# When the loads, a row store and the read-back around the expert routing are asked for, in a hybrid decoder layer on one core

## The chip, the cores and the metric

One NeuronCore of a Trainium2 chip runs the whole layer in float32. The metric is device time in microseconds (us) of one execution, lower is better; the kernel before is given as the median of three timed executions, and one more execution was profiled.

## The reference

A decoder layer over 1024 tokens of width 1024: conditioning by `c`, input projection, sparse attention beside differential attention, output projection, and then a mixture of 32 experts. Only the last part matters here:

```python
x = x + gate_a[:, None] * jnp.dot(o, w_out[l])             # the residual that is kept
h = rms_norm(x, g_moe[l]) * (1.0 + scale_m) + shift_m
# hier_moe: top-1 group of 4, then top-2 of its 8 experts; gates from two softmaxes
for e in range(N_EXPERTS):
    hid = jax.nn.silu(jnp.dot(h, w_gate[e])) * jnp.dot(h, w_up[e])
    y = y + gates[:, e:e + 1] * jnp.dot(hid, w_down[e])
x = x + gate_m[:, None] * y
return rms_norm(x, g_final)
```

## The kernel before, in words

**Stages.** Conditioning and projections, the two attentions, then three stages that matter here.

*Output projection and routing.* For each of T = 8 row tiles of 128 tokens, TensorE (PE) projects (`project_out`), VectorE (DVE) adds the residual into `XT` (the tile `X`, 8 x 1024 columns), ScalarE (ACT) writes the tile scaled by its root mean square into `h2` (L954, signal `h2_done`), PE turns the tile and ACT keeps it in `h2T`, and PE computes the router's logits from `h2T` (L1985, signal `lg_ps`). `h2` has two places, `SC[0:2048]`, and `h2T` two, `SC[2048:4096]`. Each row tile of `h2` is stored to the DRAM tensor `h2_rows` by SyncE's queue (SP, `store_h2`, L533, signal `h2_out`). From the logits, DVE and PE build a list of token rows: 20 steps of 128 rows, each step four slots of 32 rows for one expert a slot. The list is `lst` (L1452, signal `route_done` 1). While DVE works on the list PE runs matmuls without a use (`keep_warm`, L1944): 5, then 6, then 14 of them, each two instructions. After the 14, PE waits for `route_done` and for the first gathered rows.

*Experts.* For step n GpSimd (POOL) gathers 128 rows of `h2_rows` into one of two places `xg` (L707, an indirect DMA), PE turns them (L2011), ACT and DVE scale them (L969, L1538), PE multiplies by gate and up (L2024), ACT and DVE form the hidden rows (L977, L1519, L1521), PE turns them (L2033) and multiplies by down (L2047), DVE multiplies by `out_row` (L1529) and POOL scatters the result to `expert_rows` (L714). The first `ev_hid` of DVE waits for `out_row`. POOL starts the first two gathers once it has `route_done` and both counts of `h2_out` (L738 to L742); the third waits until PE has turned the first.

*Weights.* Every expert's weights come from HBM once: gate 1 MB and up 1 MB into one of 7 gate/up places, down 1 MB into one of 7 down places, all by SP's queue in a written-out order. Expert w (in the order of `SEQ`) uses place w % 7. Place 6 for gate/up is `SC[0:4096]`: gate lies in the columns of `h2`, up in those of `h2T`. Place 4 for gate/up and for down and place 5 for down lie in `X`: columns 0 to 6143 are free after the last use by expert 25, the rest after that by expert 26. Experts 23 to 25 are last used in step 15, expert 26 in step 17, experts 29 to 31 in step 19. Expert 6 is first used in step 3. A place is asked for again when PE has finished with it: gate/up after `gu_ps` (L580), down after `dn_ps` (L584). So the loads of experts 7 and 8 are the first of a stream that begins when PE has finished gate/up of step 0.

*End.* The residual was overwritten by weights, so SP reads it back as `h2_rows` into `XT` (L587 to L589, signal `x2_back`, waited for as 8 tiles by PE at the end and by DVE). When all scatters have landed (`rows_out`) SP reads the 8 MB of `expert_rows` into `yg` (L614), PE and DVE add them to the residual, ACT, POOL and DVE normalise, and SP stores the output (L617).

**The order on SP around the change** (L559 to L577): wait for the end of the projection; gate/up of expert 5; down 2; wait for `h2_done` 8 and store the last row tile; down 3; wait for `h2T_ps`; down 5; wait for both `h2_out`; wait for `lg_ps` 8; gate and up of expert 6; wait for `route_done` 1 and for the first two gathers (`xg_in`); `out_row`; down 6; then the loop over the steps.

Of the kernel before, what the change touches and what calls it, by code (L numbers as in the profile page):

```python
# [14 lines left out]
P = 128  # L15
# [9 lines left out]
def groups_of(i):  # L25

    kind, _, t = tile_at(i)
    step = 4 if kind == "diff" else 2
    return [(b, min(b + step, t + 1)) for b in range(0, t + 1, step)]
# [36 lines left out]
def hybrid_layer(nc, x, c, w_ada, b_ada, g_attn, w_in, g_kv, w_uk, w_uv, lam_q1, lam_k1, lam_q2, lam_k2,  # L66
                 g_sub, w_out, g_moe, w_group, b_group, w_router, b_router, w_gate, w_up, w_down, g_final, out):
    _, S, D = x.shape
    T = S // P
    KC = D // P  # L70
    _, NH, LAT, DH = w_uk.shape
    DV = g_sub.shape[1]
    QD = lam_q1.shape[1]
    NG = w_group.shape[2]
    NE = w_router.shape[2]
# [21 lines left out]
    DNS = 7  # L97
# [26 lines left out]
    parts, last_use = [], {}  # L124
# [24 lines left out]
    h2_dram = nc.dram_tensor("h2_rows", [S, D], F32, kind="Internal").ap()  # L149
# [4 lines left out]
    with ctx:  # L154
# [3 lines left out]
        def sem(name):  # L158
            return ctx.enter_context(nc.semaphore(name))
# [117 lines left out]
        h2 = SC[:, 0:2 * D].rearrange("p (a n) -> p a n", a=2)  # L277
# [28 lines left out]
        def dist(t):  # L306
# [42 lines left out]
        op_ps, x2_sq, h2_done = (  # L349
            sem(n) for n in ("op_ps", "x2_sq", "h2_done"))  # L350
        h2_out = [sem(f"h2_out{i}") for i in range(2)]
# [4 lines left out]
        gu_in = [sem(f"gu_in{i}") for i in range(GUS)]  # L356
# [11 lines left out]
        gu_at = [QKV[:, 0:4096], QKV[:, 6144:10240], QKV[:, 20480:24576], W7[:, :], X[:, 0:4096],  # L368
                 QKV[:, 12288:16384], SC[:, 0:4096]]
# [42 lines left out]
        wg_d = w_gate[0].rearrange("e (p c) n -> e p (c n)", c=KC)  # L412
        wu_d = w_up[0].rearrange("e (p c) n -> e p (c n)", c=KC)
# [1 line left out]
        x_d = x[0].rearrange("(t p) d -> t p d", p=P)  # L415
        win_d = w_in[0].rearrange("(j p) n -> p j n", p=P)

        def gate_up_load(sp, e, b):

            for dst, src in ((gu_at[b][:, 0:2048], wg_d), (gu_at[b][:, 2048:4096], wu_d)):  # L420
                sp.dma_start(dst, src[bass.ds(e, 1)].rearrange("o p n -> (o p) n")).then_inc(gu_in[b], 16)

        def down_load(sp, e, b):

            sp.dma_start(dn_at[b], wd_d[bass.ds(e, 1)].rearrange("o p n -> (o p) n")).then_inc(dn_in[b], 16)
# [23 lines left out]
        def _(sp):  # L449
# [80 lines left out]
            def store_h2(t):  # L530

                sp.wait_ge(h2_done, t + 1)
                sp.dma_start(h2_dram[P * t:P * (t + 1), :], h2[:, t % 2, :]).then_inc(h2_out[t % 2], 16)  # L533

            def expert_of(w):

                sp.wait_ge(eid_done, 1)
                return sp.value_load(eid[0:1, SEQ[w]:SEQ[w] + 1], min_val=0, max_val=NE - 1)

            def freed(n, places):  # L540

                return [w for w in range(places, NE) if last_use[w - places] == n]

            for t in range(SPILLED):
                if t == 1:
                    sp.wait_ge(op_ps, 2)
                    sp.dma_start(gate_late, mod_dram[:, 0:D].partition_broadcast(P).rearrange(
                        "p o (k n) -> p (o k) n", k=KC)).then_inc(out_row_in, 16)
                elif t == EARLY + 1:
                    for w in range(IN_X):  # L550
                        gate_up_load(sp, expert_of(w), w)
                        down_load(sp, expert_of(w), w)
                    sp.wait_ge(op_sb, 2 * EARLY)
                    for w in range(IN_X, IN_X + 2):
                        gate_up_load(sp, expert_of(w), w)
                store_h2(t)
            sp.wait_ge(h2T_ps, 2 * SPILLED)
            gate_up_load(sp, expert_of(4), 4)
            down_load(sp, expert_of(4), 4)  # L559
            store_h2(SPILLED)  # L560
            sp.wait_ge(op_ps, 2 * T)
            gate_up_load(sp, expert_of(5), 5)
            down_load(sp, expert_of(2), 2)
            store_h2(T - 1)
            down_load(sp, expert_of(3), 3)
            sp.wait_ge(h2T_ps, 2 * T)
            down_load(sp, expert_of(5), 5)
            for i in range(2):
                sp.wait_ge(h2_out[i], 16 * (T // 2))
            sp.wait_ge(lg_ps, T)  # L570
            gate_up_load(sp, expert_of(6), 6)
            sp.wait_ge(route_done, 1)
            for i in range(2):
                sp.wait_ge(xg_in[i], 16)
            sp.dma_start(out_row, mod_dram[:, 3 * D:4 * D].partition_broadcast(P).rearrange("p o n -> p (o n)")
                         ).then_inc(out_row_in, 16)
            down_load(sp, expert_of(6), 6)  # L577
            for n in range(NSTEP + 1):
                if n < NSTEP:
                    sp.wait_ge(gu_ps, n + 1)  # L580
                    for w in freed(n, GUS):
                        gate_up_load(sp, expert_of(w), w % GUS)
                if n >= 1:
                    sp.wait_ge(dn_ps, 2 * n)  # L584
                    for w in freed(n - 1, DNS):
                        down_load(sp, expert_of(w), w % DNS)
                    if n - 1 == last_use[max(range(5, NE, DNS))]:  # L587
                        for t in range(T):
                            sp.dma_start(XT[:, t, :], h2_dram[P * t:P * (t + 1), :]).then_inc(x2_back, 16)  # L589
            sp.wait_ge(route_done, 2)  # L590
            n_ov = sp.value_load(ovi[0:1, NOV:NOV + 1], min_val=0, max_val=NOV)
# [30 lines left out]
        def _(pool):  # L622
# [64 lines left out]
            for i, t in enumerate(sel_tiles):  # L687
                w = P * (t + 1)
                sc = SC[:, sc_off[t]:sc_off[t] + w]
                above, _, run = (a[:, 0:w] for a in sel_tmp[i % 2])  # L690
                pool.wait_ge(sel_kept, i + 1)
                link(pool.tensor_tensor(run, run, above, ALU.add))
                link(pool.tensor_scalar(run, run, -1.0, -NEG, ALU.add, ALU.mult))
                pool.tensor_tensor(sc, run, dist(t), ALU.add).then_inc(sel_done, 1)
# [73 lines left out]
        def _(act):  # L768
# [66 lines left out]
            for n in range(IH * NS):  # L835
                t = sel_tiles[n // IH]
# [11 lines left out]
            for step in range(32):  # L848
                act.wait_ge(trial_set, step + 1)
                for k in range(ONACT):  # L850
                    i, n = ONDVE + k, ONACT * step + k
                    t = sel_tiles[i]
                    w = P * (t + 1)
# [67 lines left out]
            for i in range(NA):  # L921
                n = len(groups_of(i))
# [17 lines left out]
            for t in range(T):  # L940
                act.wait_ge(x2_half, 2 * t + 2)
                if t:
                    act.wait_ge(x2_sq, t)
                if t >= 2:
                    act.wait_ge(h2_out[t % 2], 16 * (t // 2))
                act.activation(h2[:, t % 2, :], XT[:, t, :], ACT.Square, accum_out=ss[:, 2 * T + t:2 * T + t + 1]
                               ).then_inc(x2_sq, 1)
                for h in range(2):
                    act.wait_ge(h2T_ps, 2 * t + h + 1)
                    if t >= 2:  # L950
                        act.wait_ge(lg_ps, t - 1)
                    act.activation(h2T[:, t % 2, BANK * h:BANK * (h + 1)], PS[:, 4 + h, :], ACT.Copy).then_inc(h2T_sb, 1)
                act.wait_ge(rstd_done, rstd_x2 + t + 1)
                act.activation(h2[:, t % 2, :], XT[:, t, :], ACT.Copy, scale=ss[:, 2 * T + t:2 * T + t + 1]  # L954
                               ).then_inc(h2_done, 1)
            act.wait_ge(e2_in, 1)
            act.activation(gx[:, :, :], gx[:, :, :], ACT.Exp).then_inc(route_exp, 1)
            act.wait_ge(e2_in, 2)
# [37 lines left out]
            with act.If(n_ov > 0):  # L996
                with act.Fori(0, NOV // 2) as i:
                    for b in range(2):
                        with act.If(n_ov > 2 * i + b):
                            n = 2 * i + (NSTEP + b)  # L1000
# [8 lines left out]
            for t in range(T):  # L1009
                if t in mixed:  # L1010
                    i = mixed.index(t)
# [1110 lines left out]
```

## Time and profile before

| | us |
|---|---|
| median of three timed executions | 1015.87 (1013.1 to 1015.96) |
| the profiled execution, its own time | 1011.23 |
| its span, first to last instruction | 1009.4 |

| engine | busy in the span |
|---|---|
| PE matmul | 953.4 us, 94% |
| DVE | 594.8 us, 59% |
| ACT | 400.8 us, 40% |
| POOL | 119.0 us, 12% |

189.88 MB were moved by DMA at a mean of 188 GB/s over the span, and at some 420 GB/s from about 730 us to 940 us. The mean granted clock of TensorE was 0.987 of full speed. Times in rows are us from the start of the span. PEld is TensorE's weight load; "SPq" is an instruction of SP's queue, with the time that it took to issue and not the time to landing. In a row with an arrow in brackets, the number is how long the engine had been idle and the name behind the arrow is what ended it. A window's row has, after the busy time of each engine, PEclk (1.00 is the 2.4 GHz level, 0.50 the 1.2 GHz level), the mean busy share of the DMA engines, and GB/s.

### The profile page before, as it was taken

The page shows a single profiled execution, that of the slowest core. Times are in us where ns is not written, and L with a number is a line of the kernel's source. Part 1 is how long each engine was busy: PE and PEld are TensorE (multiplying, and loading weights), DVE is VectorE, ACT ScalarE, POOL GpSimd, SP SyncE. Part 2 cuts the span into 40 slices and gives each one's busy share as a digit, 9 for nine tenths or more (in the row PEclk, how much of TensorE's full clock was granted, in tenths as well). Part 3 has the DMA queues.
Part 4 walks back from the last instruction along what each step waited for, and adds up shares of the span by engine and source line. Part 5 has one row for each costly group of instructions (what it writes and reads, how often), then busy time and mean ns, then how long its engine had stood idle before and what let it go on. Part 6 is the DMA issues. An engine that isn't in the chain of part 4 may idle for free.

```text
span 1009.4 us, 15052 instructions
## 1 busy us (share of the span) xinstructions
PE 953.4 (94%) x5352; PEld 520.2 (52%) x5352; DVE 594.8 (59%) x1597; ACT 400.8 (40%) x909; POOL 119.0 (12%) x218
## 2 busy tenths in 40 slices
PE   3899999999999999999999999999899999989984
PEld 2464575444448756677766455557433434323421
DVE  3489647999999798987777234365322223312227
ACT  6130236666650488777668121212211112211113
POOL 2001000000008411110000000000111111111004
PEclk9999999999999999999999999997999999999998
DMA  9997101111111000050000410199699999999889
GB/s 325 333 358 274 43 22 32 32 42 25 39 43 27 1 1 2 1 190 2 1 2 1 167 63 22 46 412 385 252 406 421 421 417 421 420 421 419 339 334 365
DMA packets 70381, 189.88 MB, mean 188 GB/s; under 512 B 10200, under 2 KB 37136, under 8 KB 58016
## 3 DMA queue, kind: packets, MB, share of 16 engines
q1 hardware_dynamic: 62320, 171.06, 44.4%
q0 software_dynamic: 5760, 16.78, 4.2%
q10 hardware_dynamic: 2224, 1.05, 0.4%
q8 instruction: 44, 0.72, 0.3%
q14 instruction: 33, 0.27, 0.1%
HBM read 174.17 MB, written 18.89 MB: 191 GB/s over the span
## 4 chain that ended last, share of the span: by engine, by line
PE 65%; DVE 20%; DMA 6%; issue 4%; SPq 2%; ACT 1%; POOL 1%; POOLq 0%; DVEq 0%; ACTq 0%
PE PS L2024 12%; PE PS L1901 11%; DVE BIAS L1161 8%; PE PS L2047 6%; PE PS L1794 6%; PE PS L1837 5%; PE PS L1859 4%; DMA X<-in_w_down_dram 3%; PE PS L1755 3%; PE PS L1707 3%; PE PS L1854 2%; DVE X L1225 2%; PE PS L1732 2%; PE PS L2011 2%; PE PS L1672 1%
## 5 line engine op out<-in xcount | busy, mean ns | idle before, releaser
L1707 PE MATMUL PS<-HT,X 128*128 128x512 f32 x384 | 168.8, 593 | 0.0
L2024 PE MATMUL PS<-QKV,HT 128*32 128x512 f32 (+2 forms) x560 | 116.0, 607 | 6.3 <-DMA X<-in_w_up_dram 3.9
L1707 PEld LDWEIGHTS PS<-HT,X 128*128 128x128 f32 x384 | 72.5, 190 | 92.4 <-issue 92.2
L873 ACT ACTIVATE X<-X,nmx 128x128 f32<-128x128 f32 (+7 forms) x128 | 98.4, 770 | 51.6 <-DVE nmx L1225 51.0
L1901 PE MATMUL PS<-QKV,HT 128*128 128x512 f32 x256 | 113.7, 597 | 0.0
L1161 DVE TENSOR_SCALAR_CACHE_REDUCE BIAS<-SC,W 128x384 f32<-128x384 f32 (+3 forms) x128 | 96.4, 810 | 1.1
L1519 DVE TENSOR_TENSOR HT<-PS,HT 128x256 f32<-128x256 f32 x20 | 8.5, 425 | 147.8 <-ACT HT L977 147.8
L856 ACT ACTIVATE X<-SC,W 128x896 f32<-128x896 f32 x64 | 69.6, 1088 | 43.1 <-DVE W L1149 43.1
L1794 PE MATMUL PS<-QKV 64*128 64x512 f32 (+3 forms) x384 | 79.0, 517 | 1.6 <-DVE nmx L1225 1.1
L1901 PEld LDWEIGHTS PS<-QKV,HT 128*128 128x128 f32 x256 | 47.4, 190 | 53.7 <-issue 53.6
L1837 PE MATMUL PS<-ident,X 128*128 128x128 f32 x432 | 63.2, 279 | 2.2 <-DVE X L1243 2.1
L977 ACT ACTIVATE HT<-PS 128x256 f32<-128x256 f32 x20 | 7.7, 384 | 138.7 <-PE PS L2024 138.7
L2024 PEld LDWEIGHTS PS<-QKV,HT 128*32 128x32 f32 (+2 forms) x560 | 32.7, 119 | 53.8 <-issue 50.3
L1225 DVE CUSTOM_DVE_ANT_0 X<-PS,R 128x128 f32<-128x128 f32 (+7 forms) x80 | 50.8, 674 | 14.6 <-PE PS L1794 8.6
L2047 PE MATMUL PS<-QKV,HT 128*32 128x512 f32 (+2 forms) x272 | 56.2, 616 | 2.9 <-DMA X<-in_w_down_dram 2.4
L1837 PEld LDWEIGHTS PS<-ident,X 128*128 128x128 f32 x432 | 47.2, 141 | 11.4 <-issue 8.7
L1225 DVE CUSTOM_DVE_ANT_0 X<-PS,SC 128x1024 f32<-128x1024 f32 (+5 forms) x48 | 42.0, 887 | 17.9 <-PE PS L1794 17.8
L2024 PE MATMUL PS<-W,HT 128*32 128x512 f32 (+2 forms) x144 | 51.0, 619 | 0.0
L1529 DVE TENSOR_TENSOR HT<-PS,R 128x512 f32<-128x512 f32 x40 | 27.7, 692 | 32.3 <-PE PS L2047 28.4
L1794 PEld LDWEIGHTS PS<-QKV 64*128 64x128 f32 x384 | 31.6, 185 | 27.8 <-issue 20.4
L2024 PE MATMUL PS<-X,HT 128*32 128x512 f32 (+1 forms) x128 | 44.1, 609 | 0.0
L1053 DVE SCALAR_TENSOR_TENSOR QKV<-QKV,cact 128x512 f32<-128x512 f32 x56 | 42.1, 752 | 2.0
(306 smaller groups left out, 1533.7 us busy)
## 6 DMA issues: line engine op xcount, KB each, us to landing
QKV<-in_w_down_dram SPq DMA_DIRECT2D x20, 1024.0 KB
QKV<-in_w_gate_dram SPq DMA_DIRECT2D x19, 1024.0 KB
QKV<-in_w_up_dram SPq DMA_DIRECT2D x19, 1024.0 KB
QKV<-in_w_ada_dram SPq DMA_DIRECT2D x8, 2048.0 KB, 14.5
QKV<-in_w_ada_dram SPq DMA_DIRECT2D x8, 1024.0 KB, 12.8
X<-in_w_in_dram SPq DMA_DIRECT2D x16, 512.0 KB, 3.8
X<-in_w_down_dram SPq DMA_DIRECT2D x8, 1024.0 KB, 28.0
QKV<-expert_rows SPq DMA_DIRECT2D x16, 512.0 KB, 10.7
```

The costliest lines, as they stand in the source:

```text
L856: act.activation(RL[:, n % 2, 0:w], SC[:, sc_off[t]:sc_off[t] + w], ACT.Sign, bias=tk[:, 4, i:i + 1].bitcast(F32), scale=-1.0, accum_out=c ...
L873: act.activation(sc, sc, ACT.Exp, bias=nmx[:, i % 4, m:m + 1], scale=-1.0, accum_out=rs[:, i, m:m + 1]).then_inc(exp_done, 1)
L1053: link(dve.scalar_tensor_tensor(out=w[:, 0, :], in0=w[:, j, :], scalar=cact[:, j:j + 1], in1=w[:, 0, :], op0=ALU.mult, op1=ALU.add))
L1161: dve.tensor_scalar(BIAS[:, i % 3, 0:w], SC[:, sc_off[t]:sc_off[t] + w], thr.bitcast(F32)[:, i:i + 1], 0.0, ALU.is_lt, ALU.add, accum_out= ...
L1225: dve.tensor_tensor_reduce(sc_buf[i % 4][:, m, 0:w], PS[:, 2 * m:2 * m + 2, :].rearrange("p a n -> p (a n)")[:, BANK * n:BANK * n + w], aw ...
L1707: end = pe.matmul(PS[:, 2 * b + half, :], WS[:, b, j, :], HT[:, j, BANK * half:BANK * (half + 1)], start=(j == 0), stop=(j == KC - 1))
L1794: end = pe.matmul(PS[:, 2 * m + n + c0 // BANK, 0:c1 - c0], QKV[rows_m, q0:q0 + P], QKV[rows_m, k0 + c0:k0 + c1], start=True, stop=True)
L1837: end = pe.transpose(PS[:, 4 + g % 2, c0:c0 + P], sc_buf[i % 4][:, m, P * b:P * (b + 1)], ident[:, :])
L1859: end = pe.matmul(PS[DH * m:DH * (m + 1), 6 + h % 2, slot], vd[:, b, v0:v0 + DH], turned_at(i)[:, g % 4, c0:c0 + P], start=(b == 0), stop= ...
L1901: end = pe.matmul(PS[:, n % 4, :], HT[:, k, P * (n // 2):P * (n // 2 + 1)], wo[:, k, BANK * (n % 2):BANK * (n % 2 + 1)], start=(k == 0), s ...
L2024: end = pe.matmul(PS[at, 2 + b, :], hgT[b][:, P * c_ + at.start:P * c_ + at.stop], WGU[w][:, c_, :, :], start=(c_ == 0), stop=(c_ == KC - 1))
L2047: end = pe.matmul(PS[at, 5 + h, :], hidT[b][:, P * c_ + at.start:P * c_ + at.stop], WDN[w][:, c_, BANK * h:BANK * (h + 1)], start=(c_ == 0 ...
```

## The change

Four edits, all in who asks for a transfer and when. No computation changes.

1. The store of the last row tile of `h2` moves from SP's queue to ACT's, right behind the ACT instructions that make it. SP keeps the wait for `h2_done` 8, now behind down 3 instead of ahead of it.
2. SP's wait for both `h2_out` moves from ahead of the loads of expert 6 to behind its waits for the first two gathers.
3. Of expert 6's gate/up place, up (the half in the columns of `h2T`) is still asked for behind `lg_ps` 8; gate (the half in the columns of `h2`) is asked for behind the first two gathers and `out_row`.
4. The read-back of the residual is asked for in two steps: 6 tiles behind the down loads that the end of step 15 frees, 2 tiles at the end of step 17, instead of all 8 at the end of step 17.

```diff
-        def gate_up_load(sp, e, b):
+        def gate_up_load(sp, e, b, halves=(0, 1)):
-            for dst, src in ((gu_at[b][:, 0:2048], wg_d), (gu_at[b][:, 2048:4096], wu_d)):
-                sp.dma_start(dst, src[bass.ds(e, 1)].rearrange("o p n -> (o p) n")).then_inc(gu_in[b], 16)
+            for h in halves:
+                sp.dma_start(gu_at[b][:, 2048 * h:2048 * (h + 1)], (wg_d, wu_d)[h][bass.ds(e, 1)].rearrange("o p n -> (o p) n")
+                             ).then_inc(gu_in[b], 16)
...
             gate_up_load(sp, expert_of(5), 5)
-            down_load(sp, expert_of(2), 2)
-            store_h2(T - 1)
-            down_load(sp, expert_of(3), 3)
+            for w in range(2, 4):
+                down_load(sp, expert_of(w), w)
+            sp.wait_ge(h2_done, T)
             sp.wait_ge(h2T_ps, 2 * T)
             down_load(sp, expert_of(5), 5)
-            for i in range(2):
-                sp.wait_ge(h2_out[i], 16 * (T // 2))
             sp.wait_ge(lg_ps, T)
-            gate_up_load(sp, expert_of(6), 6)
+            gate_up_load(sp, expert_of(6), 6, (1,))
             sp.wait_ge(route_done, 1)
             for i in range(2):
                 sp.wait_ge(xg_in[i], 16)
+            for i in range(2):
+                sp.wait_ge(h2_out[i], 16 * (T // 2))
             sp.dma_start(out_row, mod_dram[:, 3 * D:4 * D].partition_broadcast(P).rearrange("p o n -> p (o n)")
                          ).then_inc(out_row_in, 16)
+            gate_up_load(sp, expert_of(6), 6, (0,))
             down_load(sp, expert_of(6), 6)
...
-                    if n - 1 == last_use[max(range(5, NE, DNS))]:
-                        for t in range(T):
+                    back = {last_use[25]: range(0, 6), last_use[26]: range(6, T)}
+                    if n - 1 in back:
+                        for t in back[n - 1]:
                             sp.dma_start(XT[:, t, :], h2_dram[P * t:P * (t + 1), :]).then_inc(x2_back, 16)
...
+            act.wait_ge(h2_done, T)
+            act.dma_start(h2_dram[P * (T - 1):P * T, :], h2[:, (T - 1) % 2, :]).then_inc(h2_out[(T - 1) % 2], 16)
             act.wait_ge(e2_in, 1)
```

## Rows read from the trace of the kernel before

**Rows 1.** Chain of waits, 690 to 740 us (start, us, what).
```profile
693.87 3.63 PE PS L1985 x16
...
709.38 6.08 DMA HT<-h_rows,SC
...
715.59 1.14 PE PS L2011 x8
...
718.37 8.41 PE PS L2024 x64
...
729.54 7.07 PE PS L2024 x64
```
**Rows 2.** Timeline of PE and of POOL, 694 to 742 us.
```profile
708.09 6.29 PE L1944 MATMUL PS<-HT,ident 128*128 128x256 f32 x28
...
711.00 0.99 POOL L707 DMA_INDIRECT HT<-h_rows,SC  x1 [0.31 <-issue]
```
**Rows 3.** Timeline of SP's queue, 695 to 730 us.
```profile
695.00 0.33 SPq L533 DMA_DIRECT2D h_rows<-SC  x1
...
705.09 0.34 SPq L421 DMA_DIRECT2D SC<-in_w_gate_dram  x1
705.53 0.38 SPq L421 DMA_DIRECT2D SC<-in_w_up_dram  x1
716.77 0.33 SPq L575 DMA_DIRECT2D R<-modulation_row  x1
...
727.86 0.35 SPq L421 DMA_DIRECT2D QKV<-in_w_gate_dram  x1
```
**Rows 4.** Windows, 690 to 727 us.
```profile
690.00:709.40 19.40, 17.71 (x111) 15.67 (x110) 12.68 (x57) 3.60 (x7) 0.80 (x3) 0.74 0.97 375
709.40:716.70 7.30, 6.08 (x32) 4.99 (x30) 0.86 (x5) 0.00 (x0) 2.28 (x2) 1.00 0.73 277
717.00:722.00 5.00, 3.63 (x24) 1.01 (x28) 2.87 (x14) 2.60 (x5) 0.99 (x1) 0.66 0.73 243
722.00:727.00 5.00, 5.00 (x50) 1.44 (x40) 0.00 (x0) 0.19 (x1) 0.00 (x0) 1.00 0.46 178
```
**Rows 5.** Page, what DMA moved in 40 slices of 25.2 us.
```profile
GB/s 325 333 358 274 43 22 32 32 42 25 39 43 27 1 1 2 1 190 2 1 2 1 167 63 22 46 412 385 252 406 421 421 417 421 420 421 419 339 334 365
```
**Rows 6.** Waits, 880 to 972 us (who waited for whom: sum, times, longest).
```profile
PE PS L2024 <- DMA X<-in_w_up_dram: 3.9, 1, 3.9
PE PS L2047 <- DMA X<-in_w_down_dram: 2.4, 1, 2.4
```
**Rows 7.** Waits of SP's queue, 690 to 760 us.
```profile
SPq L574 <- DMA HT<-h_rows,SC: 10.8, 1, 10.8
SPq L537 <- DMA h_rows<-SC: 6.6, 1, 6.6
```
**Rows 8.** Timeline of ACT, 694 to 742 us.
```profile
708.67 0.23 ACT L957 ACTIVATE gx<-gx 128x32 f32<-128x32 f32 x1 [13.70 <-DVE gx L1455]
```
**Rows 9.** Line 2024, its matmuls on place 6 (form, ns min/median/max, first and last start).
```profile
L2024 PE MATMUL PS<-SC,HT x112: 592/592/643, 753.8 to 937.1; 128*32 128x512 f32 x96, 128*64 128x512 f32 x16
```
**Rows 10.** Timeline of SP's queue and of PE, 917 to 974 us.
```profile
919.37 2.54 SPq L421 DMA_DIRECT2D W<-in_w_up_dram  x1
922.74 9.79 SPq L425 DMA_DIRECT2D QKV<-in_w_down_dram  x3
953.92 4.14 SPq L589 DMA_DIRECT2D X<-h_rows  x8
...
969.78 3.70 PE L2085 MATMUL PS<-X,ident 128*128 128x512 f32 x8 [0.58 <-DMA X<-h_rows]
```
**Rows 11.** Chain of waits, 893 to 975 us.
```profile
893.57 31.12 DMA X<-in_w_down_dram
...
954.23 7.00 PE PS L2024 x64
...
970.74 3.32 DMA expert_rows<-HT,SC
```

## The prediction

> **What bounds the kernel now.** I read the chain of waits first, around the change. With the list of rows ready, POOL's first gather is issued at 709.38 us and lands 6.08 us later, at 715.46; PE starts to turn the rows at 715.59, multiplies by gate and up of step 0 from 718.37 for 8.41 us, and step 1 follows at 729.54 [rows 1]. So the first gather is on the path. Then the timeline of PE: what it does meanwhile is the filler of 14, from 708.09 for 6.29 us, to 714.38 [rows 2]. PE could not turn earlier than 714.38 however soon the rows came. The idle time that a faster gather can take away is 715.59 - 714.38 = 1.21 us, and no more.
>
> Next the stretch behind it. From about 733 us DMA moves 417 to 421 GB/s slice after slice [rows 5], and PE waits for weights twice near the end of that stretch, 3.9 and 2.4 us [rows 6]. The load that ended the second wait was asked for at 893.57 and took 31.12 us [rows 11]: a queue of 31.12 x 0.42 = 13 MB stood before it. The middle of the expert part is therefore bound by the stream of weights, and the stream begins at 727.86, when PE has done gate and up of step 0 and its places are asked for again [rows 3]. What moves the end of step 0's gate/up moves the stream and everything behind it, one for one, as long as the DMA engines are free when it begins.
>
> Last the tail: SP asks for the expert rows when the last scatter has landed, 970.74 + 3.32 = 974.1 [rows 11]. Only what moves that scatter moves the tail.
>
> **Part 1, the loads ahead of the gather (edits 1 to 3).** Removed from ahead of the gathers: gate of expert 6, 1 MB, asked for at 705.09 [rows 3]. Also removed: SP's wait of 6.6 us for the row store [rows 7], so that up of expert 6 is asked for at about 697.6, when the last logits are done (693.87 + 3.63 [rows 1]), instead of 705.53, and down 3 and down 5 come a little sooner. How much is queued when the gather starts? From 709.4 to 716.7, when the second gather lands, DMA moved 7.3 x 277 = 2.02 MB [rows 4]. Two gathers are 1.05 MB, so 0.97 MB were loads still waiting. Before 709.4 DMA was 97% busy [rows 4], so asking sooner alone gains nothing; it is the 1.05 MB taken out that empties the queue, just in time. With it empty the two gathers have 0.97 / 0.42 = 2.3 us less ahead of them. The second lands at 714.4, and the first, 1.2 us ahead of it as before, at 713.2, an issue-to-landing of 3.8 us.
>
> That price has no row of its own. The bounds are 3.32 us, a scatter of the same size with little else in flight [rows 11], and 5.7 us, the second gather itself (711.00 [rows 2] to about 716.7, the end of SP's wait [rows 3, 7]), most of whose time was behind the last loads already. At 3.8 the gather lands 1.2 us inside the filler; at 5.7 it lands at 715.1. I take 3.8, nearer to the lower end, since the loads left were over half of what stood ahead. The gain is 1.2 us at 3.8, and (6.08 - 5.7) = 0.4 us at 5.7.
>
> By the Trainium skill ("DMA: Bandwidth & Descriptors", the anatomy of one DMA on the GpSimd path) such a transfer costs about 2.0 us plus its bytes at 436 GB/s, which is an estimate of 3.2 us for 512 KB. The sum would be 1.2 us by that too; the scatter's 3.32 agrees with it and the gather's 5.7 does not.
>
> **The clock.** In 717 to 722 us the granted clock was 0.66 on average: it fell to the 1.2 GHz level behind PE's 1.21 us of waiting, a turn of 1.14 us, and 1.6 us of waiting for ACT and DVE [rows 1, 4]. Gate/up of step 0 took 8.41 us, that of step 1, at the full level, 7.07: the fall costs 1.34 us [rows 1]. The change removes the first of the two waits, not the second. From below the gain is 0, from above 1.34. Between gate/up of step 0 and of step 1 (726.8 to 729.54) PE has breaks too and keeps the clock; what is left here stands between the two cases. I leave it at 0 in the sum and make the other value a rival.
>
> **What is added behind the gather.** Gate 6 (1.05 MB, 2.5 us of DMA) now stands between `out_row` and down 6, asked for at about 715. Expert 6 is first multiplied at 753.8 [rows 9], so it has 38 us. `out_row` is asked for no later than before, and DVE needs it only behind step 0's gate/up, at 727. The one thing that could be hit is the start of the stream. DMA was idle for 27% of 717 to 722 and for 54% of 722 to 727 [rows 4], 4.1 us, and 0.9 us more to 727.86; a stream that begins 1.2 us sooner leaves 3.8, against 2.5 needed. Cost 0. Without that cover it would be up to 2.5.
>
> **The store on ACT's queue (edit 1).** One issue on ACT, about 0.35 us as SP's issues are, in a gap of 13.70 us [rows 8]; behind it only the two exponentials wait, due at 708.67. Cost 0. POOL needs the store landed before it issues at 709.38. On SP's queue it took from 695.00 to about 704, where SP's wait of 6.6 us ended [rows 3, 7], behind the loads asked for before it. It has 13.5 us from 695.2, so 0; if it were held until the SP queue had drained (about 709) it would land near 710.5 and cost up to 2 us. By the Trainium skill (same page, "Issuing engines are not separate DMA queues") transfers of different engines share the same DMA engines and interleave, so the move itself saves nothing and the store is not held; no row of before has a store on ACT's queue.
>
> **SP's waits.** `h2_done` now stands behind down 3, and nothing but down 5 and up 6 is queued behind it; both had to wait for that anyway. The wait for `h2_out` behind the gathers is met on arrival, since the gathers themselves needed it.
>
> **Part 2, the read-back (edit 4).** Six of eight tiles (3.15 MB, 7.5 us) are asked for behind the down loads freed by step 15, issued from 922.74 for 9.79 us, so near 932 instead of 953.92 [rows 10]. They queue behind the last weights and fill DMA time of which the page shows some to spare (339 GB/s in the slice from 933) [rows 5]. What was late: PE's first addition of the residual waited 0.58 us [rows 10]. But its next additions wait for the last scatter, landed at 974.1 [rows 11], and 969.78 + 3.70 = 973.5 was already sooner. The last scatter took 3.32 us, our lower bound. Gain 0, from above 0.3 us.
>
> **Sum.** 1.2 + 0 + 0 = 1.2 us less. Against the profiled execution: 1011.23 - 1.2 = 1010.0 (span 1009.4 to 1008.2). That execution lies 4.6 us under the median of the timed ones, so I carry the difference and not the level: 1015.87 - 1.2 = 1014.7.
>
> **Rivals.** (a) *The clock holds too*: 1.2 + 1.34 = 2.5 us less, 1013.3. For it: only one break is left. Against: that one was the longer. 0.26. (b) *The gather is slow by itself*, 5.7 us: 0.4 us less, 1015.5; in effect the change does not do what it says. For it: the second gather. 0.18. (c), on the other side: *The read-back takes DMA time from the last weights*: up of expert 31 was asked for at 919.37; with the lag of 31.12 it lands at about 950.5, and step 19 wants it at 954.23 [rows 10, 11]. If the 3.15 MB went ahead of or among the weights, all would land 7.5 us later, of which 3.7 over the margin, and 1.3 more for a fall of the clock. It decides once over 3.7 us (1.6 MB) of read-back pass in front. Then + 5.0 - 1.2: 1019.7. Against it: the same queue of SP carries both, weights first. 0.08. (d) Something not in these rows, more often a gain (a wait on the stream that shrinks) than a loss: 0.12. My forecast case: 0.36.
>
> **Range and chances.** A measurement of this kernel tells about 0.3%, 3.05 us, from no change; the three timed executions alone span 2.9 us. (a) less 1.5 gives 1011.8, (b) plus 1.5 gives 1017.0. Over 3.05 us faster: part of (a) and (d), and little of the forecast, 0.27. Slower: (c) and a little of (b) and (d), 0.11. Within: 0.62.
>
> **What would show it.** Right: in the profile after, PE's idle time ahead of the first turn is gone or under 0.2 us; the first gather takes 3.5 to 5 us; SP asks for `R` sooner than 716.77; gate/up of step 0 takes 8.4 (forecast) or 7.1 us (rival a); the distance from its end to the end of the span is the same within 0.5 us. Wrong: a gather of over 5.5 us (b); a wait of PE on `W`, `QKV` or `BIAS` weights between 935 and 965 us (c); POOL's first gather issued later than some 0.9 us behind the list (the store); DMA still full when the stream begins.

## The result, and the profile after

| | before | after |
|---|---|---|
| median of six timed executions each, us | 1015.91 (1013.1 to 1016.11) | 1008.36 (1007.32 to 1010.08) |
| profiled execution, own time, us | 1011.23 | 1009.45 |
| its span, us | 1009.4 | 1007.7 |

The ratio is 0.9934 with a 95% interval of [0.9917, 0.9951]: 7.5 us less by the medians, where 1.2 were forecast. Two later jobs with the unchanged after gave 0.9951 [0.9935, 0.9967] and 0.9962 [0.9948, 0.9977], so some 0.5%, 4 to 7.5 us, is the size to explain. All three ratios lie beyond the 0.3% from which a gain was to be told, though the interval of the last reaches down to 0.23%. Here and below ratios are of fast executions alone; two slow ones, 1245.56 us with the read-back alone and 3218.31 us with both halves behind the gathers, are left out of them.

The two profiled spans differ by 1.7 us only. The two executions were not alike ahead of the change: the last logits start at 697.12 in the one after, at 693.87 in the one before [rows 1], and nothing that PE waits for was changed before that point. So the traces are compared from that start on. First the chain of waits after, 690 to 740 us (start, us, what), the part that answers to [rows 1]:

```profile
697.12 3.35 PE PS L1990 x16
...
711.04 5.19 DMA HT<-h_rows,SC
...
716.37 1.14 PE PS L2016 x8
...
719.16 7.12 PE PS L2029 x64
```

and PE's own timeline, with its idle time before an instruction in brackets:

```profile
709.76 6.29 PE L1949 MATMUL PS<-HT,ident 128*128 128x256 f32 x28
716.37 1.13 PE L2016 MATMUL PS<-ident,HT 128*128 128x128 f32 x8 [0.33 <-DMA HT<-h_rows,SC]
719.16 7.07 PE L2029 MATMUL PS<-QKV,HT 128*32 128x512 f32 x64 [1.66 <-ACT HT L974]
```

Three things are to be seen. The gather takes 5.19 us instead of 6.08. PE's wait for it is 0.33 instead of 1.21 us, where the prediction wanted none or under 0.2. Gate/up of step 0 takes 7.07 instead of 8.4 us. And one thing was not in the prediction at all: from the start of the last logits to the gather's issue it is 711.04 - 697.12 = 13.9 us, against 709.38 - 693.87 = 15.5 before. That stretch computes the token list. The change puts one issue into it, in a gap of ACT, and its length turns out to differ between executions of one kernel.

SP's queue after, 695 to 730 us, which answers to [rows 3]:

```profile
701.21 0.34 SPq L421 DMA_DIRECT2D SC<-in_w_up_dram  x1
718.04 0.33 SPq L576 DMA_DIRECT2D R<-modulation_row  x1
719.13 0.34 SPq L421 DMA_DIRECT2D SC<-in_w_gate_dram  x1
720.25 0.34 SPq L426 DMA_DIRECT2D BIAS<-in_w_down_dram  x1
727.02 0.34 SPq L421 DMA_DIRECT2D QKV<-in_w_gate_dram  x1
```

Up of expert 6 is asked for 4.1 us behind the start of the last logits, where it was 705.53 - 693.87 = 11.7 us; gate comes behind the gathers; the stream of weights begins at 727.02. The DMA engines just before that:

```profile
723.00:727.00 4.00, 4.00 (x39) 1.62 (x32) 0.18 (x1) 0.38 (x1) 0.00 (x0) 1.00 1.00 409
```

They were 100% busy up to the stream's start, where in the kernel before they had been 46% busy in 722 to 727 [rows 4]. "DMA still full when the stream begins" was one of the prediction's signs of being wrong.

ACT issues the store of the last row tile in 0.35 us, in a gap of 12.13 us; the store landed 8.5 us later, at about 707, well ahead of the gather's issue:

```profile
698.24 0.35 ACTq L960 DMA_DIRECT2D h_rows<-SC  x1
710.34 0.23 ACT L962 ACTIVATE gx<-gx 128x32 f32<-128x32 f32 x1 [12.13 <-DVE gx L1460]
```

Toward the end, PE's waits from 880 to 972 us, which answer to [rows 6]:

```profile
PEld PS L2090 <- DMA X<-h_rows: 4.9, 1, 4.9
PE PS L2090 <- DMA X<-h_rows: 4.0, 1, 4.0
PE PS L2029 <- DMA X<-in_w_up_dram: 3.9, 1, 3.9
PE PS L2052 <- DMA X<-in_w_down_dram: 1.3, 1, 1.3
```

The stream still makes PE wait for as long as before (3.9 us), as it should if both moved together; the wait for down is 1.3 instead of 2.4 us. The read-back, asked for 21 us sooner against the end of the last down matmul, is waited for longer than before, not shorter. Edit 4 is not the reason: in two later profiles without it, the gate half alone and edits 1 to 3 again, the wait is as long.

```profile
PE PS L2087 <- DMA X<-h_rows: 4.4, 1, 4.4
PE PS L2089 <- DMA X<-h_rows: 4.6, 1, 4.6
```

### The profile page after: what moved, and what is told of

Same layout as the page of the kernel before. It is cut to its first block, busy times and chain, and to the rows that moved or that the text cites. A ratio compares the mean times of both kernels' runs of the same rounds, so it can differ in the third digit from the quotient of the medians.

```text
span 1007.7 us, 15056 instructions
## 1 busy us (share of the span) xinstructions
PE 954.2 (95%) x5352; PEld 521.1 (52%) x5352; DVE 594.5 (59%) x1597; ACT 400.9 (40%) x909; POOL 118.2 (12%) x218
## 4 chain that ended last, share of the span: by engine, by line
PE 65%; DVE 20%; DMA 6%; issue 4%; SPq 2%; ACT 1%; POOL 1%; POOLq 0%; DVEq 0%; ACTq 0%
PE PS L2029 12%; PE PS L1906 11%; DVE BIAS L1166 8%; PE PS L2052 6%; PE PS L1799 6%; PE PS L1842 5%; PE PS L1864 4%; DMA X<-in_w_down_dram 3%; PE PS L1760 3%; PE PS L1712 3%; PE PS L1859 2%; DVE X L1230 2%; PE PS L1737 2%; PE PS L1677 2%; PE PS L2016 2%
## 5 line engine op out<-in xcount | busy, mean ns | idle before, releaser
L2029 PE MATMUL PS<-QKV,HT 128*32 128x512 f32 (+2 forms) x560 | 115.6, 599 | 6.3 <-DMA X<-in_w_up_dram 3.9
L2029 PEld LDWEIGHTS PS<-QKV,HT 128*32 128x32 f32 (+2 forms) x560 | 32.7, 117 | 53.7 <-issue 50.2
L2052 PE MATMUL PS<-QKV,HT 128*32 128x512 f32 (+2 forms) x272 | 54.5, 595 | 1.8 <-DMA X<-in_w_down_dram 1.3
## 6 DMA issues: line engine op xcount, KB each, us to landing
QKV<-in_w_up_dram SPq DMA_DIRECT2D x19, 1024.0 KB, 20.9
```

What stands on the lines that cost most here:

```text
L2029: end = pe.matmul(PS[at, 2 + b, :], hgT[b][:, P * c_ + at.start:P * c_ + at.stop], WGU[w][:, c_, :, :], start=(c_ == 0), stop=(c_ == KC - 1))
L2052: end = pe.matmul(PS[at, 5 + h, :], hidT[b][:, P * c_ + at.start:P * c_ + at.stop], WDN[w][:, c_, BANK * h:BANK * (h + 1)], start=(c_ == 0 ...
```

## The experiments

Two theories stood first: the gain is at the start of the expert part (the gather and the clock), or it is in the tail (the read-back). Every job, of two to four kernels, also ran executions of before on the same chip; ratios are against those.

**The kernel before, again.** No edit.

> The kernel before, unchanged, for a second profile. The median of before (1015.9) is 4.7 us above its profiled execution (1011.23), and the change measured 7.5 us, six times the forecast. Theory 1 (clock): the usual execution of before has more falls of TensorE's clock than the profiled one, so this profile shows a time near 1015.9 and, against the first, 2 to 5 us more at the 1.2 GHz level, with the waits on DMA the same. Theory 2 (tail): the usual execution loses its extra time behind the last down matmul, where the read-back, the last scatters and the reads of the expert rows meet: the distance from there to the end, 40.2 us in the first profile, is then 43 us or more. Time against before: the same.

Ratio 1.0004 [0.9986, 1.0022]. Its profiled execution took 1013.9 us of span, 4.5 more than the first profile of the same kernel. The granted clock in 40 slices of 25 us (page), in the first profile and in the second:

```profile
PEclk9999999999999999999999999997999999999998
PEclk9999999999999899999999999997999999999998
```

One window, in the first and in the second:

```profile
345.00:355.00 10.00, 9.44 (x53) 5.14 (x51) 9.24 (x44) 9.17 (x38) 1.89 (x6) 1.00 0.00 1
345.00:355.00 10.00, 10.00 (x35) 5.66 (x37) 7.38 (x33) 7.87 (x33) 1.29 (x3) 0.51 0.00 0
```

At 345 us, in the attention, the granted clock of the second profile was 0.51 for ten us, the 1.2 GHz level; in the first it was 1.00. By the last logits this execution was 2.9 us later (696.81 against 693.87). Theory 1 named this; the tail was 41.6 us against 40.2, not the 43 of theory 2. Over two jobs 67 executions of the kernel before took 1009.5 to 1019.0 us, and the profiled one was among the luckier. Where the clock falls is part of that scatter; whether it is all of it was not tried. It is no gain: it hits both kernels.

**The read-back alone** (edit 4 in the kernel before).

```diff
-                    if n - 1 == last_use[max(range(5, NE, DNS))]:
-                        for t in range(T):
+                    back = {last_use[25]: range(0, 6), last_use[26]: range(6, T)}
+                    if n - 1 in back:
+                        for t in back[n - 1]:
```

> Before, with edit 4 alone: read-back in two steps. Theory 1 (the gain is at the start of the expert part: gather and clock): within 1 us of before, 1015 to 1016. Theory 2 (the gain is in the tail): 4 to 6 us less, 1010 to 1012. Prediction on record: 0 to 0.3 us less.

Ratio 1.0007 [0.9995, 1.002]: nothing that can be told, as the prediction said. But its trace held the key to the rest. Here the list was early, and the old order of loads stood unchanged (chain, 690 to 735 us; PE's waits in the same stretch):

```profile
709.44 8.74 DMA HT<-h_rows,SC
718.31 1.96 PE PS L2012 x8
721.92 9.65 PE PS L2025 x64
```

```profile
PE PS L2012 <- DMA HT<-h_rows,SC: 3.9, 1, 3.9
```

The gather was issued 12.7 us behind the start of the last logits (696.76), 2.8 us earlier than in [rows 1], and took 8.74 us instead of 6.08. It landed at the same distance. The early list was worth nothing. From 709 to 717 us DMA moved 3.2 MB, of which the two gathers are 1.05: the loads ahead of the gather had not drained.

**Edits 1 to 3 without the read-back.** The diff of the change less its edit 4.

> Before, with edits 1 to 3 alone: store on ACT's queue, gate of expert 6 behind the gathers; the read-back stays in one step. Theory 1: nearly all of the gain, 6 to 7.5 us less, 1008.5 to 1010. Theory 2: 1.2 to 2.5 us less, 1013.4 to 1014.7, as forecast for this part.

Ratio 0.9953 [0.9938, 0.9969], 4.8 us: more than theory 2 and less than theory 1 gave, but all of the gain that the later jobs found for the whole change. In its profile the list was late (issue 15.5 us behind the logits), the gather took 4.6 us, PE had no idle time ahead of the turn, and gate/up took 7.07 us.

**A filler of 17.** In the kernel before:

```diff
-            keep_warm(14)
+            keep_warm(17)
```

> Before, with 17 instead of 14 useless matmuls between the token list and the first gathered rows, so that PE runs on to about 715.7 us, 0.15 us past the landing of the gather at 715.46, and has no idle time there. Loads, store and read-back stay. It tries the clock by itself. Theory 1: the clock stays at 2.4 GHz through gate/up of step 0 (7.07 instead of 8.41 us), 1.2 us less in the profile and a good part of the gain in the median. Theory 2: the same as before or 0.2 us more.

Ratio 1.0007 [0.9996, 1.0019]. It did not try what it was meant to. The list was early here too, the gather took 8.81 us, PE waited 2.65 us for it behind the longer filler, and gate/up took 9.9 us. As a second case of an early list with the old order it confirms the one above: the turn began 21.57 us behind the logits, there 21.55.

With this the theory became: *Q, a queue*. In the old order the gather's landing is set by the loads ahead of it, wherever the list is ready; the change takes one of them away and asks for the other sooner, so the gather follows the list.

**The store alone** (edit 1).

```diff
-            store_h2(T - 1)
             down_load(sp, expert_of(3), 3)
+            sp.wait_ge(h2_done, T)
...
+            act.wait_ge(h2_done, T)
+            act.dma_start(h2_dram[P * (T - 1):P * T, :], h2[:, (T - 1) % 2, :]).then_inc(h2_out[(T - 1) % 2], 16)
```

> Before, with edit 1 alone: the last row tile is stored by ACT's queue and SP waits for h2_done behind down 3; gate and up of expert 6 still ahead of the gather, both behind h2_out. Theory Q: DMA was 97% busy there and the same bytes stand ahead of the gather, so the first gather still lands 21 to 21.6 us after the start of the last logits, and the time is within 0.1% of before. Rival S (SP's wait for the store was what made the loads late): half or more of the gain, ratio 0.997 or less.

Ratio 0.9996 [0.998, 1.0012]. Turn 20.85 us behind the logits, up to 0.9 sooner than the old order, gate/up 9.78 us, no gain in time that can be told. Rival S is not borne out.

**The gate half alone** (edits 2 and 3, the store still on SP's queue).

```diff
-            for i in range(2):
-                sp.wait_ge(h2_out[i], 16 * (T // 2))
             sp.wait_ge(lg_ps, T)
-            gate_up_load(sp, expert_of(6), 6)
+            gate_up_load(sp, expert_of(6), 6, (1,))
...
+            for i in range(2):
+                sp.wait_ge(h2_out[i], 16 * (T // 2))
...
+            gate_up_load(sp, expert_of(6), 6, (0,))
             down_load(sp, expert_of(6), 6)
```

> Before, with edits 2 and 3 alone: gate of expert 6 behind the gathers, the store still by SP. Theory Q: nearly all of the gain of edits 1 to 3, ratio 0.9955 to 0.997, first gather landing 19 to 20.3 us after the start of the last logits where the clock is low during the list for 6.8 to 10.2 us. Rival S: within 0.1% of before.

Ratio 0.9972 [0.9958, 0.9986], turn at 19.50 us, gate/up 7.07 (PE's timeline):

```profile
714.96 1.13 PE L2013 MATMUL PS<-ident,HT 128*128 128x128 f32 x8 [0.54 <-DMA HT<-h_rows,SC]
717.74 7.07 PE L2026 MATMUL PS<-QKV,HT 128*32 128x512 f32 x64 [1.65 <-ACT HT L971]
```

These two edits together carry most of the gain, if not all. They take gate away from ahead of the gather and also let up be asked for some 6 us sooner (5 us behind the start of the last logits instead of 11); neither was run without the other, so their shares are not shown. Whether the store adds something to it (0.9972 against 0.9953 with it) lies within the two intervals and stays open.

**The change again.**

> The changed kernel, unchanged, timed beside its parts. The first job gave ratios of 0.9953 for edits 1 to 3 without the read-back and 1.0007 for the read-back alone; the change measured 0.9934. Theory Q (queue: all of the gain is that the first gather no longer stands behind loads): 0.995, the read-back adds nothing. Rival R (the read-back adds something once the start is earlier): 0.9935.

Ratio 0.9951 [0.9935, 0.9967]. Its profile shows the early list with the new order (PE's and POOL's timelines, 686 to 745 us):

```profile
693.78 1.98 PE L1990 MATMUL PS<-wgr,SC 128*128 128x36 f32 x16 [1.05 <-ACT SC L955]
...
711.95 1.13 PE L2016 MATMUL PS<-ident,HT 128*128 128x128 f32 x8 [0.46 <-DMA HT<-h_rows,SC]
714.74 7.07 PE L2029 MATMUL PS<-QKV,HT 128*32 128x512 f32 x64 [1.66 <-ACT HT L974]
```

```profile
706.49 1.31 POOL L710 DMA_INDIRECT HT<-h_rows,SC  x1 [12.79 <-DVE SC L1457]
```

Issue 12.7 us behind the logits as in the read-back experiment, landing 5.3 us later instead of 8.7, turn at 18.2 instead of 21.55.

**Both halves behind the gathers**, in the changed kernel.

```diff
             sp.wait_ge(lg_ps, T)
-            gate_up_load(sp, expert_of(6), 6, (1,))
             sp.wait_ge(route_done, 1)
...
-            gate_up_load(sp, expert_of(6), 6, (0,))
+            gate_up_load(sp, expert_of(6), 6)
```

> The changed kernel, with up of expert 6 also asked for behind the gathers, directly after gate. Ahead of the gather stand 1 MB (2.5 us) less again. Theory Q: in executions where the list is ready early (clock low for 3.4 us only in that stretch) the gather gains up to 2.5 us more, in the others PE is held by its own filler and nothing is gained, so 0 to 1 us less than the changed kernel; first gather from issue to landing under 4.5 us. Rival: 4.6 MB behind the gathers no longer fit ahead of the stream of weights, which then starts late: 0.5 to 2 us more than the changed kernel.

Ratio 0.9961 [0.9945, 0.9977]; with after at 0.9951 in the same job, no further gain that can be told, and no loss either. The gather took 4.6 us, PE's filler ended last, and PE's waits from 880 to 930 us show where the DMA time was missed:

```profile
PE PS L2028 <- DMA X<-in_w_up_dram: 5.5, 1, 5.5
```

5.5 us for the stream where it is 3.7 to 4.4 in every other profile. From the end of gate/up of step 0 to the last down matmul this kernel needs 241.7 us, after 240.6. That is the rival's mechanism, a stream that is served later, and in this profile it costs 1.1 us; the rival's 0.5 to 2 us more in the ratio is within the intervals and not shown.

**A shorter filler in the changed kernel**, to try the clock without touching the queue.

```diff
-            keep_warm(14)
+            keep_warm(10)
```

> The changed kernel with 10 instead of 14 useless matmuls ahead of the gathered rows: PE's filler ends 1.8 us sooner, the gather is untouched. It tries the clock without the queue. Theory C (part of the gain is that the clock no longer falls at step 0): PE idle 1.5 to 2.5 us ahead of the turn, clock falls, gate/up of step 0 takes 8.4 to 9.9 us instead of 7.07, and the time is 1.0 to 2.5 us more than the changed kernel (1009.8), 1010.8 to 1012.3. Theory without C (only the landing of the gather counts): gate/up 7.07, the time within 0.5 us of the changed kernel or less where the filler was the last to end.

Ratio 0.998 [0.9968, 0.9992]: of the change's 0.4 to 0.7% about half or more is given back. PE's timeline:

```profile
709.60 4.56 PE L1949 MATMUL PS<-HT,ident 128*128 128x256 f32 x20
716.10 1.12 PE L2016 MATMUL PS<-ident,HT 128*128 128x128 f32 x8 [1.93 <-DMA HT<-h_rows,SC]
718.88 8.77 PE L2029 MATMUL PS<-QKV,HT 128*32 128x512 f32 x64 [1.65 <-ACT HT L974]
```

The turn begins 19.3 us behind the logits, just as in after (19.25). Only the clock differs: PE idle 1.93 us instead of 0.33, and gate/up takes 8.77 instead of 7.07 us. That is 1.7 us in this execution. By the ratios, 0.998 against 0.9951 and 0.9962 of after in other jobs, it is 1.8 to 2.9 us, an estimate across jobs; the interval of 0.9962 overlaps this one. So the fall costs about what it lengthens gate/up by, or somewhat more.

**A longer filler in the kernel before**, 20 instead of 14.

> Before, with 20 instead of 14 useless matmuls there, enough to bridge the wait for the gather also where the list is ready early (the first try, with 17, met a gather of 8.8 us and left PE idle for 2.65 us). Theory C: gate/up of step 0 takes 7.07 us; where the list is early (turn at 21.5 us after the last logits' start) that is 1.3 to 2.8 us less than before, where it is late the filler itself delays the turn by up to 1.8 us; median 0 to 1.5 us less than before. Theory without C: 0 to 1.8 us more than before.

Ratio 1.0005 [0.999, 1.002]. Inconclusive: the filler ended at 716.77, the gather landed at 716.90 and PE waited 0.26 us, less than in after, yet the clock fell and gate/up took 8.77 us. Filling up to a late gather bought nothing that can be told, and a short wait alone does not settle whether the clock holds.

**The change and the change without its edit 4, in one job.**

> The changed kernel, unchanged, beside the same without the split read-back, in one job. If the read-back adds nothing (as it did alone, 1.0007) the two ratios agree within their intervals, both 0.9935 to 0.996. If it adds where the start is early, this one is 0.15% or more below the other.

> Edits 1 to 3 without edit 4 (the read-back in one step at the end of step 17), as in the first job, where the ratio was 0.9953. Nothing from the read-back: 0.9935 to 0.996, equal to the changed kernel of this job within the intervals. Rival: 0.15% or more above it.

Ratios 0.9962 [0.9948, 0.9977] and 0.9961 [0.9947, 0.9975]: the same. The split read-back adds nothing that can be told, alone or with the rest.

All profiles in one table, in us behind the start of the last logits; the rows are sorted by when the list was ready. "Last down" is from the end of gate/up of step 0 to the end of the last down matmul.

| kernel | gather issued | turn begins | gate/up takes | gate/up ends | last down | tail |
|---|---|---|---|---|---|---|
| *gate 6 ahead of the gathers* | | | | | | |
| filler 17 | 12.6 | 21.6 | 9.9 | 34.2 | 240.7 | 42.0 |
| read-back alone | 12.7 | 21.6 | 9.6 | 34.8 | 240.5 | 41.2 |
| filler 20 | 14.0 | 21.8 | 8.8 | 33.4 | 240.6 | 41.9 |
| store alone | 14.1 | 20.9 | 9.8 | 33.4 | 240.8 | 42.4 |
| before | 15.5 | 21.7 | 8.4 | 32.9 | 242.5 | 40.2 |
| before, again | 15.6 | 21.2 | 8.7 | 32.7 | 242.8 | 41.6 |
| *gate 6 behind the gathers* | | | | | | |
| after, third | 12.6 | 18.2 | 7.1 | 28.0 | 240.5 | 41.1 |
| after, again | 12.7 | 18.2 | 7.1 | 28.0 | 240.6 | 41.2 |
| after | 13.9 | 19.3 | 7.1 | 29.1 | 240.6 | 40.9 |
| edits 1 to 3, again | 13.9 | 19.3 | 7.1 | 29.2 | 240.8 | 41.6 |
| gate half alone | 14.0 | 19.5 | 7.1 | 29.4 | 240.3 | 41.5 |
| after, filler 10 | 14.1 | 19.3 | 8.8 | 30.9 | 240.5 | 41.1 |
| both halves behind | 14.1 | 18.9 | 7.1 | 28.7 | 241.7 | 41.5 |
| edits 1 to 3 | 15.5 | 20.3 | 7.1 | 30.1 | 242.5 | 40.9 |

How late the list is goes with the clock: in the 15 us behind the start of the last logits the granted clock was at the 1.2 GHz level for some 3 us where the gather is issued at 12.6 or 12.7, for some 7 us at 13.9 to 14.1, and for some 10 us at 15.5 or 15.6, in either half of the table.

In the upper half the turn begins at 20.9 to 21.8 us whatever the list does; in the lower half it follows the list, at 18.2 to 20.3. Where the list is early the change gains 3.4 us there, in the middle 1.4 to 2.5, where it is late 0.9 to 1.4. The gate/up that follows is 1.3 to 2.8 us shorter on top. Together 2.6 to 6.8 us at the end of gate/up of step 0. Behind that point "last down" is 240.3 to 240.8 us in both halves of the table, but for both halves behind (241.7) and the three kernels with the latest list (242.5 to 242.8). Those three share a wait of 2.2 to 2.4 us for down weights near 925 us, where the others have 0.5 to 1.6, and behind it the clock was at the 1.2 GHz level for some three us; why that wait goes with a late list was not tried. With a list as late, the length is the same with and without the change, which is why the gain arrives at the end whole.

## Why the prediction was wrong, point by point

Two terms of the sum were too small: the first, the idle time that a faster gather takes away (1.2 us), and the clock, put at 0. The path was right.

**The bound that failed** was in the first part: "The idle time that a faster gather can take away is 715.59 - 714.38 = 1.21 us, and no more". It was true of the one execution profiled. The end of the filler is not fixed: it runs behind the list, and the list was as late there as in any profile (15.5 us, with ten us at the 1.2 GHz level from the last logits on). With an earlier list the same filler ended 2.8 us sooner, and the gather, held by the loads, did not. So the term was mis-sized: 1.2 us in the sum, 0.9 to 3.4 us on the chip. The mechanism behind it, loads that stand ahead of the gather, was right: edits 2 and 3 alone show it. That it is the megabyte of gate and not also the sooner asking for up ("asking sooner alone gains nothing") was argued and not run.

**The clock** was left "at 0 in the sum", and 1.34 was made rival (a), with a chance of 0.26. In the profiles with the gate half behind the gathers and the filler left at 14 gate/up took 7.07 us, seven of seven; in the six with it ahead 8.4 to 9.9, none at the full level. The term is 1.3 to 2.8 us. The shorter filler brings the fall back with the gather untouched and loses time, so the clock is a cause of the gain and not a companion. How the change holds the clock is open: less idle time ahead of the turn fits the shorter filler (1.93 us, fallen) and not the filler of 20 (0.26 us, fallen as well). The upper bound was also too low, again because one execution stood for all.

**The price of a gather** was taken as 3.8 us, between 3.32 and 5.7. It measured 4.6 to 5.4 in the profiles of the new order. With the filler of 14 PE waited for it 0.54 us at most, so this error was small, but the side chosen was wrong. The estimate of 3.2 us by the Trainium skill ("DMA: Bandwidth & Descriptors", the anatomy of one DMA on the GpSimd path) lies below all of them; the row of the second gather, 5.7, was the better guide.

**Range and median.** The working said that the profiled execution lay 4.6 us under the median and carried the difference on. It should have asked what the other executions do that this one does not. The range of 1011.8 to 1017.0 was built from scatter around terms of one execution and left out the first result, 1008.36, and the later medians of after as well, 1009.8 and 1011.0.

**The free DMA time ahead of the stream** was counted as 3.8 us against 2.5 needed. In after there was none left: the engines were full from 723 to the stream's start at 727.02. The working had moved the stream by 1.2 us only. From SP's request for `R` to the stream's start it is 727.02 - 718.04 = 8.98 us, where it was 727.86 - 716.77 = 11.09 [rows 3]: 2.1 us less, for gate/up was shorter too. That the term's cost was still 0 is partly luck: "last down" is no longer than in the old order with the same list, and one more megabyte (both halves behind) lengthened it by 1.1 us.

**What held.** The stream of weights begins when gate/up of step 0 ends and passes the gain on one for one, kernels with a list as late compared. The distance from there to the end of the span was to be the same within 0.5 us; it is 281.5 after against 282.7 before, but edits 1 to 3, whose list was as late as before's, have 283.4, so the shorter distance goes with the earlier list and not with the change. Gate of expert 6 behind the gathers cost nothing that can be seen. The store on ACT's queue cost nothing and was not late. The read-back gained nothing. Rival (c), weights delayed by the read-back, did not happen: in after PE waited for no weights behind 925 us. Rival (b), a gather that is slow by itself, was right in part in the duration, 4.6 to 5.4 us where it had 5.7, and wrong in what follows.

## What to carry to other kernels

Before bounding a term by the idle time in one trace, ask whether both ends of that idle time move together from one execution to the next; here one followed the list and the other a queue of loads. Here a transfer on the critical path gained when a megabyte that was not needed yet was asked for behind it; a second megabyte moved there gained no more and began to cost the stream. And filler that keeps the clock up must not end too soon: in the changed kernel 1.8 us less of it gave back about half of the gain or more. To reach the event is not enough, as the filler of 20 in the kernel before shows.

## What the runs showed of the hardware that was not expected

- One unchanged kernel on one core took 1009.5 to 1019.0 us, and part of it can be seen as stretches at the 1.2 GHz level that come and go: ten us at 345 us in the second profile of before, none there in the first.
- The clock can be low while PE has work without a break: from 694 to 704 us in the first profile of before PE was busy for all of the 10 us, with the small matmuls of the routing and with fillers, and the granted clock was 0.50.
- A fall of the clock is not told by the length of one wait. In after, PE idle for 0.33 and then 1.66 us around the turn kept the full level (716 to 719 us); in the kernel before with a filler of 20, 0.26 and 1.66 us did not.
- The read-back asked for 21 us sooner did not land sooner in the profile after: PE waited 4.0 us for it at its first addition, against 0.58 before [rows 10]. In those two profiles it was hidden behind the last scatter. The wait is not the split's: in two profiles with the read-back in one step it was 4.4 and 4.6 us, and in the second of them the chain of waits ran through it (issued at 954.10, 16.19 us to landing). Why eight transfers asked for from 930 to 952 us are complete only near 971 us in after, with DMA 56% busy from 960 to 965 us, was not tried.
